# Score products of neighbouring units issued in turn in the second block's mixers

## The chip, the cores and the metric

The program runs on one core of a Trainium2 chip. Its metric is the device time of one execution, in microseconds; the median of the runs is compared. TensorE (PE in the profile) does the matrix products, VectorE (DVE) and ScalarE (ACT) the elementwise work, GpSimd (POOL) very little, and SyncE (SP) issues the DMAs of the weights.

## What is computed

A row block x of 256 tokens by 1024 features goes through two model blocks of two layers each. The first block (a stick-breaking and gated linear mixer, then a routed set of experts) isn't touched by the change. The second block does, for each of its two layers:

```
h    = rms_norm(x) * gain
proj = h @ w_in                                   # split into the inputs of four branches
y_a  = latent attention, 4 heads of 64+32         # softmax over 256 keys
y_b  = differential attention, 4 heads, two softmaxes each, w = p0 - lam * p1
y_c  = banded attention with sinks, 4 query heads
y_d  = neighbourhood attention with a bias table, 4 heads
x    = x + concat(norm(y_a), y_b, norm(y_c), norm(y_d)) @ w_out
x    = x + square(relu(rms_norm(x) @ w_up)) @ w_down
```

Everything is fp32. The large products are done as three products of values split into a high and a low part (fp32r); the products of the attentions are plain fp32 products. The profile shows a plain one as two pairs of weight load and matmul, called two passes below.

## The kernel before

All weights stream once through a ring of four slots of 1 MB. ScalarE copies each slot's tile to a rounded high part (line 926 inside the mixers) and VectorE subtracts it from the raw tile to get the low part (line 935); TensorE waits for the low part. Three split tiles are held, so a split waits until the tile three before it has been used.

The attention of a layer of the second block ("mix2") is cut into 20 **units**, each with 128 queries, 256 keys and two heads (branches A, C and D) or the two softmaxes of one head (branch B). A unit is written here as its branch, its p and its i, so B01 is branch B, p = 0, query half i = 1. The units in order (B00, B01, B10, ... B31, A00, ... A11, C00, ... C11, D00, ... D11) are dealt to three **lanes** in turn, and each lane has its own PSUM bank and its own buffers; a unit starts only when the one before it in its lane has been written out.

The steps of a unit are, on TensorE, **S** (two score products of 128 queries by 256 keys, lines 1861 to 1863), **T** (transposes of the probabilities, line 1871) and **V** (the products with v, line 1877); on ScalarE **exp** (line 2005) and **cpT** (the copy of the transposes, line 2011); on VectorE **max** (lines 2162 to 2171: mask, row maximum, scaling), **rec** (line 2175 to 2183: reciprocals, for B the difference of the softmaxes) and **y** (line 2191, for B line 2188: the output of the unit).

The contraction of a score product is over 64 rows in the branches B, C and D, and over 96 in A. With 64 rows it lies in rows 0 to 63 of the array if p is even and in rows 64 to 127 if p is odd, because `rows64 = slice(64 * p, 64 * p + 64)`, and `slice(64 * (p % 2), ...)` for B.

When the units of a branch are done, its **fin** steps run. For branch C these are facC on ScalarE (line 2069: squares, then a logarithm and an exponential that make the norm's factor), finC2 on VectorE (line 2264: the branch times its factor), finC.T on TensorE (line 1957: transposes), turnC on ScalarE (line 2081: the high part of the transposed branch) and finC3 on VectorE (line 2269: its low part). The output projection runs in four tiles out2.0 to out2.3, each in two halves c0 and c1 (line 1840, 12 matmuls each half). out2.0 takes branch B, out2.1 branch A, out2.2 branch C, and out2.3 branch D. A tile's first half waits for the fin3 step of its branch: `pe.wait_ge(v_ms, 19 * l + (11, 16, 18, 19)[t])`. The input projection runs in the steps in2.0 to in2.5 (lines 1792 and 1816), and the steps named mla (lines 1912 to 1929) lift the queries and keys of branch A.

Each engine executes its instructions in program order. For TensorE, ScalarE and VectorE that order is written out by hand: a string of digits for each layer and engine, in which each digit says which of several generators goes on to its next `yield`. The digits 1 to 3 are the three lanes, 0 and 4 (and 5) the projection, the fin steps and the weight splits.

```python
def steps(order, *lanes):

    live = dict(enumerate(lanes))
    for q in [int(q) for q in order]:
        if q in live and next(live[q], 0) == 0:
            del live[q]
```

Of the kernel before, what the change touches and what calls it, by code (L numbers as in the profile page):

```python
# [12 lines left out]
ACT = mybir.ActivationFunctionType  # L13
# [11 lines left out]
IN1 = (0, 1, 3, 2, 4, 5)  # L25
ORDER = {("mix1", 0, "PE"): "00400400066550500556650155301535005500515534505314540151315050543510455510404545050055044500000", ("mix1", 0, "ACT"): "0000040660004056645103500061563500543100153113156000135051005640040504400", ("mix1", 0, "DVE"): "00006006040606664065666510630004650031040513141600450044004653415400440044500",
# [3 lines left out]


def layout(parts):
# [86 lines left out]
def program(nc, a, out):  # L119
    ctx = ExitStack()  # L120
    with ctx:
# [1728 lines left out]
        def pe_units(pe, l, L):  # L1850
            for n, u in enumerate(L.units):
                at = len(L.units) * l + n
                if n:
                    pe.wait_ge(L.vector, 3 * at)
                if n == 0 or L.units[n - 1].br != u.br:
                    pe.wait_ge(v_ms, 19 * l + {"A": 8, "B": 3, "C": 14, "D": 9}[u.br])
                    pe.wait_ge(a_ev, 6 * l + {"A": 2, "B": 3, "C": 3, "D": 6}[u.br])
                    pe.wait_ge(v_ev, 10 * l + {"A": 5, "B": 3, "C": 3, "D": 10}[u.br])
                    if u.br == "A":
                        pe.wait_ge(a_ms, 13 * l + 5)  # L1860
                for j, (q, k) in enumerate(u.qk):
                    ins = pe.matmul(ps[:, L.b, 256 * j:256 * j + 256], q, k, start=True, stop=True)  # L1862
                ins.then_inc(L.psum, 1)
                yield
                if u.br == "B":
                    pe.wait_ge(L.vector, 3 * at + 2)
                else:
                    pe.wait_ge(L.scalar, 2 * at + 1)
                for j in range(len(u.vs)):
                    for kt in range(2):  # L1870
                        ins = pe.transpose(ps[:, L.b, 256 * j + 128 * kt:256 * j + 128 * kt + 128], L.pt[:, j, 128 * kt:128 * kt + 128], ident)  # L1871
                ins.then_inc(L.psum, 1)
                yield
                pe.wait_ge(L.scalar, 2 * at + 2)
                for j, c in enumerate(u.vs):
                    for kt in range(2):
                        ins = pe.matmul(ps[:, L.b, 64 * j:64 * j + 64], L.ptT[:, j, kt, :], m2.v[:, kt, c:c + 64], start=(kt == 0), stop=(kt == 1))  # L1877
                ins.then_inc(L.psum, 1)
                yield
# [83 lines left out]
        def pe_mix2(pe, g, l):  # L1963
            pe_x_T(pe, 4 + 2 * l)
            if l == 0:
                pe_spin(pe, 6, 2)
            steps(ORDER["mix2", l, "PE"], pe_main2(pe, g, l), *(pe_units(pe, l, L) for L in LANES), pe_misc2(pe, l))
# [654 lines left out]
```

## Time and profile before

| what | value |
|---|---|
| median of 3 runs | 1470.93 us (1469.54 to 1472.16) |
| profiled execution: its own time | 1464.29 us |
| profiled execution: span of the core | 1462.1 us |
| busy: PE, PEld, DVE, ACT, POOL | 1317.6, 983.6, 729.3, 526.4, 49.6 us |
| mean granted TensorE clock | 0.960 |
| mixer of layer 0 of the second block | some 122 us, from 827 to 949 us |
| mixer of layer 1 of the second block | some 124 us, from 1149 to 1273 us |

Times are microseconds from the first instruction. A matmul's end in the profile is modelled, since matmuls are pipelined: the time that a step takes of TensorE is read from the first start in it to the first start in the next step, not from its length. PEld is the weight load that goes ahead of each matmul. A name such as "ps<-ar" says which tile is written and which are read; "ar" is the common scratch area, and "gate" holds, in the branch B, the keys of the second softmax.

### The profile page before, as it was taken

To read this page: it belongs to the slowest core of one execution; us is meant where nothing else is said; L and a number is where in the kernel's file an instruction comes from. 1 tells how busy PE (TensorE), PEld (TensorE's weight loads), DVE (VectorE), ACT (ScalarE), POOL (GpSimd) and SP (SyncE) were. 2 spreads that over 40 slices of the span, in tenths; PEclk is the share of its full clock that TensorE was granted. 3 is DMA by queue.
4 is the path that set the end of the run, shared out by engine and by line. 5 is a ranking of instruction groups with operands and counts; after the bars stand their busy time and mean duration, and the time that the engine had idled before them with its cause. 6 is when DMAs were issued, how large, how long until landed. Compare 5 with 4: busy or idle time off the path is not lost. (4 is left out here: it accounts for less than half of the span.)

```text
span 1462.1 us, 21540 instructions
## 1 busy us (share of the span) xinstructions
PE 1317.6 (90%) x9066; PEld 983.6 (67%) x9066; DVE 729.3 (50%) x1126; ACT 526.4 (36%) x894; POOL 49.6 (3%) x46
## 2 busy tenths in 40 slices
PE   5999998867689999976776999999999999999997
PEld 2766774433247667643432878799988978799996
DVE  1744653122157367421111878764554777755454
ACT  3545331000045344200001546554444546644343
POOL 0200000000002000000000110000000110000000
PEclk9999999889899999998888999999999999999999
DMA  9799899999977958999999705446655404455550
GB/s 354 284 332 312 334 403 420 421 422 421 419 278 285 337 188 331 421 421 421 421 421 402 187 6 202 146 154 209 191 187 150 108 32 171 144 174 200 180 200 39
DMA packets 135975, 392.08 MB, mean 268 GB/s; under 512 B 26816, under 2 KB 40128, under 8 KB 111296
## 3 DMA queue, kind: packets, MB, share of 16 engines
q1 hardware_dynamic: 132128, 389.48, 71.5%
q10 hardware_dynamic: 3744, 1.15, 0.4%
q8 instruction: 75, 1.23, 0.3%
q14 instruction: 28, 0.23, 0.0%
HBM read 389.45 MB, written 1.05 MB: 267 GB/s over the span
## 5 line engine op out<-in xcount | busy, mean ns | idle before, releaser
L421 DVE TENSOR_TENSOR spl<-ring,spl 128x2048 fp32r<-128x2048 f32 x65 | 149.0, 2292 | 135.7 <-ACT spl L412 135.7
L545 PEld LDWEIGHTS ps<-hh,spl 128*128 128x128 f32 x1728 | 204.1, 189 | 6.9 <-issue 5.8
L545 PE MATMUL ps<-hh,spl 128*128 128x256 f32 x1728 | 206.2, 281 | 2.8 <-DVE hh L507 2.8
L412 ACT ACTIVATE spl<-ring 128x2048 fp32r<-128x2048 f32 x66 | 126.6, 1919 | 148.1 <-PE ps L545 107.7
L2349 PE MATMUL ps<-spl,ur 128*128 128x512 f32 x768 | 176.7, 389 | 0.0
L1348 PE MATMUL ps<-ring,ar 128*32 128x256 f32 x960 | 112.7, 486 | 63.3 <-DMA spl_as_slots<-in_w_up 28.6
L2349 PEld LDWEIGHTS ps<-spl,ur 128*128 128x128 f32 x768 | 143.2, 188 | 29.2
L935 DVE TENSOR_TENSOR spl<-ring,spl 128x1024 fp32r<-128x1024 f32 (+2 forms) x120 | 138.2, 1175 | 23.0 <-ACT spl L926 22.6
L1348 PE MATMUL ps<-spl_as_slots,ar 128*32 128x256 f32 x736 | 110.5, 486 | 28.3 <-DMA spl_as_slots<-in_w_up 17.3
L926 ACT ACTIVATE spl<-ring 128x1024 fp32r<-128x1024 f32 (+2 forms) x120 | 116.7, 1010 | 43.3 <-PE ps L525 10.7
L1348 PEld LDWEIGHTS ps<-ring,ar 128*32 128x32 f32 x960 | 54.7, 139 | 101.9 <-issue 95.7
L525 PE MATMUL ps<-spl,hh 128*128 128x512 f32 x480 | 117.6, 398 | 3.6 <-DVE hh L1048 1.3
L1561 DVE TENSOR_TENSOR ar<-ps,ar 128x256 f32<-128x256 f32 x16 | 6.8, 425 | 220.1 <-ACT ar L1437 220.1
L525 PEld LDWEIGHTS ps<-spl,hh 128*128 128x128 f32 x480 | 88.4, 188 | 32.0 <-issue 12.2
L1437 ACT ACTIVATE ar<-ps 128x256 f32<-128x256 f32 x16 | 6.1, 383 | 276.6 <-PE ps L1348 276.6
L1348 PEld LDWEIGHTS ps<-spl_as_slots,ar 128*32 128x32 f32 x736 | 52.5, 139 | 52.8 <-issue 44.7
L1816 PE MATMUL ps<-hh,spl 128*128 128x256 f32 (+1 forms) x672 | 86.0, 286 | 2.0 <-DVE hh L507 1.9
L1816 PEld LDWEIGHTS ps<-hh,spl 128*128 128x128 f32 (+1 forms) x672 | 81.2, 191 | 6.9 <-issue 6.0
L1393 PE MATMUL ps<-spl_as_slots,ar 128*32 128x512 f32 x400 | 58.1, 594 | 10.0 <-ACT ar L1450 8.1
L606 PE MATMUL ps<-ring,ccol 128*32 128x512 f32 x384 | 52.1, 639 | 14.9 <-DMA ring<-in_w_ada 14.9
L1413 PE MATMUL ps<-gate,hh_as_floats 128*128 128x512 f32 x128 | 63.0, 614 | 1.9 <-ACT hh_as_floats L1446 1.7
L1339 PE MATMUL ps<-ar,xn 128*128 128x256 f32 (+1 forms) x320 | 58.3, 340 | 0.0
(370 smaller groups left out, 1787.8 us busy)
## 6 DMA issues: line engine op xcount, KB each, us to landing
ring<-in_w_up SPq DMA_DIRECT2D x58, 1024.0 KB, 5.8
spl_as_slots<-in_w_down SPq DMA_DIRECT2D x50, 1024.0 KB, 16.8
ring<-in_w_ada SPq DMA_DIRECT2D x48, 1024.0 KB, 7.1
ring<-in_w_down SPq DMA_DIRECT2D x40, 1024.0 KB, 4.9
ring<-in_w_in SPq DMA_DIRECT2D x34, 1024.0 KB, 7.5
ring<-in_w_gate SPq DMA_DIRECT2D x34, 1024.0 KB, 15.9
spl_as_slots<-in_w_up SPq DMA_DIRECT2D x30, 1024.0 KB, 16.7
ring<-in_w_out SPq DMA_DIRECT2D x16, 1024.0 KB, 7.7
```

The source lines that it names most:

```text
L412: sc.activation(t.hi, t.raw, ACT.Copy).then_inc(s_hi, 2)
L421: v.tensor_tensor(t.lo, t.raw, t.hi, ALU.subtract).then_inc(s_lo, 1)
L525: ins = pe.matmul(ps[:, banks[i], 0:cn], le, ri, start=(kk == 0 and q == 0), stop=(kk == 7 and q == 2), skip_group_check=True)
L545: ins = pe.matmul(ps[:, banks[m // 2], (m % 2) * 256:(m % 2) * 256 + 256], le, ri, start=(kk == 0 and q == 0 and m % 2 == 0), stop=(kk == ...
L926: sc.activation(t.hi[:, h], t.raw[:, h], ACT.Copy).then_inc(s_hi, 1)
L935: ins = v.tensor_tensor(t.lo[:, h], t.raw[:, h], t.hi[:, h], ALU.subtract)
L1339: ins = pe.matmul(slots_out(c, k), xn[:, i, 128 * k:128 * k + 128], mo.pr[:, i, s0:s0 + n], start=(i == 0), stop=(i == 1), skip_group_chec ...
L1348: ins = pe.matmul(ps[32 * j:32 * j + 32, 2 + q % 2, 256 * z:256 * z + 256], mo.xg[c][:, k, CAP * e - CHUNKS[c][0]:CAP * e - CHUNKS[c][0] + ...
L1393: ins = pe.matmul(ps[32 * j:32 * j + 32, c, :], mo.aT[q % 2][:, f, 32 * j:32 * j + 32], T["down", l, 4 * q + j].raw[:, f, 512 * c:512 * c ...
L1413: pe.matmul(ps[:, 6 + m % 2, :], mo.pT[:, q, 128 * i:128 * i + 128], mo.ys[:, 512 * c:512 * c + 512], start=True, stop=True).then_inc(s_b, 1)
L1816: ins = pe.matmul(o, le, ri, start=(kk == 0 and q == 0 and m % 2 == 0), stop=(kk == 7 and q == 2), skip_group_check=True)
L2349: ins = pe.matmul(ps[:, 2 * cc + i, :], le, ri, start=(d == 0 and f2 == 0 and f == 0 and q == 0), stop=(d == 7 and f2 == 1 and f == 1 and ...
```

## The change

A unit's S step gets two yields in place of one, so that another generator can come between its two score products. The semaphore that VectorE waits for is still raised by the second product alone.

```diff
                 for j, (q, k) in enumerate(u.qk):
                     ins = pe.matmul(ps[:, L.b, 256 * j:256 * j + 256], q, k, start=True, stop=True)
-                ins.then_inc(L.psum, 1)
-                yield
+                    if j:
+                        ins.then_inc(L.psum, 1)
+                    yield
```

The strings of the two layers get the extra digits for TensorE. In four places of each layer two units of opposite rows then follow each other in turn: B01 with B10, B30 with B21, C10 with D00, and D10 with D01. Everywhere else s0 and s1 of a unit stay together. Decoded into steps, these are the places where the order differs (s0 and s1 are the two products of S; the rest of the order is the same in both kernels):

```
layer 0, PE, before: B00.S B01.S B10.S in2.2
             after:  B00.s0 B00.s1 B01.s0 B10.s0 B01.s1 B10.s1 in2.2
         before: mla.q B30.S B20.T B21.S mla.qperm
         after:  mla.q B30.s0 B21.s0 B30.s1 B21.s1 B20.T mla.qperm
         before: C11.T C10.S C11.V finA.T D00.S out2.0c0 out2.0c1 D00.T C10.T D10.S C10.V
                 out2.1c0 D10.T D01.S D00.V D10.V D11.S finC.T out2.1c1 D01.T out2.2c0 out2.2c1
                 D11.T D01.V D11.V finD.T out2.3
         after:  C11.T C10.s0 D00.s0 C10.s1 D00.s1 C11.V finA.T out2.0c0 out2.0c1 D00.T C10.T
                 out2.1c0 C10.V D00.V D10.s0 D01.s0 D10.s1 D01.s1 out2.1c1 D10.T D11.s0 D11.s1
                 D10.V finC.T out2.2c0 D01.T out2.2c1 D11.T D01.V D11.V finD.T out2.3
layer 0, ACT, before: D00.cpT split D10.exp split D10.cpT facC D01.exp turnC split D11.exp
             after:   D00.cpT split split D10.exp D01.exp D10.cpT facC turnC split D11.exp
layer 0, DVE, before: C10.rec D10.max split D00.rec C10.y D01.max D00.y finC2 D11.max finC3
             after:   C10.rec split D00.rec C10.y D00.y D10.max D01.max finC2 D11.max finC3
layer 1, PE, before: B00.S B01.S B10.S in2.2
             after:  B00.s0 B00.s1 B01.s0 B10.s0 B01.s1 B10.s1 in2.2
         before: B10.V B30.S B20.T B21.S B20.V mla.qperm
         after:  B10.V B20.T B30.s0 B21.s0 B30.s1 B21.s1 B20.V mla.qperm
         before: C11.T C10.S D00.S C11.V finA.T out2.0c0 out2.0c1 D10.S C10.T D00.T
                 out2.1c0 C10.V D00.V D01.S out2.1c1 D10.T finC.T D11.S D10.V D01.T out2.2c0
         after:  C11.T C10.s0 D00.s0 C10.s1 D00.s1 C11.V finA.T out2.0c0 out2.0c1 C10.T D00.T
                 out2.1c0 C10.V D00.V D10.s0 D01.s0 D10.s1 D01.s1 out2.1c1 D10.T finC.T D11.s0
                 D11.s1 D10.V D01.T out2.2c0
layer 1, ACT, before: D00.exp split C10.cpT D10.exp D00.cpT facC split D01.exp D10.cpT turnC
             after:   D00.exp split C10.cpT D00.cpT facC split D10.exp D01.exp D10.cpT turnC
layer 1, DVE, before: C10.rec split D10.max split C10.y D00.rec D10.rec D00.y D01.max finC2 split finC3
             after:   C10.rec split split D00.rec C10.y D00.y D10.max D01.max D10.rec finC2 split finC3
```

## Rows read from the trace of the kernel before

**Rows 1.** The page's first part: busy us (share of the span) and instructions.

```profile
PE 1317.6 (90%) x9066; PEld 983.6 (67%) x9066; DVE 729.3 (50%) x1126; ACT 526.4 (36%) x894; POOL 49.6 (3%) x46
```

**Rows 2.** Stretches, both mixers: busy us (x) by engine, PEclk, DMA share, GB/s.

```profile
826.90:949.50 122.60, 120.46 (x753) 101.16 (x752) 93.50 (x197) 66.82 (x173) 6.47 (x5) 0.99 0.40 128
1149.00:1273.00 124.00, 121.16 (x755) 101.60 (x754) 94.46 (x198) 67.76 (x173) 6.33 (x5) 0.99 0.38 124
```

**Rows 3.** Timeline of PE, layer 0, B00, B01, B10: start, us, engine line op.

```profile
834.97 0.70 PE L1862 MATMUL ps<-ar 64*128 64x256 f32 x2
...
835.93 0.70 PE L1862 MATMUL ps<-ar 64*128 64x256 f32 x4
836.37 0.70 PE L1862 MATMUL ps<-gate,ar 64*128 64x256 f32 x4
837.00 4.40 PE L1816 MATMUL ps<-hh,spl 128*128 128x256 f32 x36
```

**Rows 4.** Timeline of PE, layer 0, B21.S and mla.qperm.

```profile
861.04 0.70 PE L1862 MATMUL ps<-ar 64*128 64x256 f32 x2
...
862.09 1.91 PE L1919 MATMUL ps<-ar 32*32 32x256 f32 x8
```

**Rows 5.** Timeline of PE, layer 0, from C10.S to D11.T.

```profile
909.58 1.13 PE L1862 MATMUL ps<-ar 64*128 64x256 f32 x4
910.63 1.10 PE L1877 MATMUL ps<-ar,xn 128*128 128x64 f32 x8
...
913.17 5.74 PE L1840 MATMUL ps<-spl,ur 128*128 128x512 f32 x24
918.75 0.60 PE L1871 MATMUL ps<-cst,xn 128*128 128x128 f32 x4
...
926.12 2.00 PE L1877 MATMUL ps<-ar,xn 128*128 128x64 f32 x16
...
929.24 0.66 PE L1957 MATMUL ps<-cst,gate 128*128 128x128 f32 x4
...
932.86 5.74 PE L1840 MATMUL ps<-spl,hh 128*128 128x512 f32 x24
938.44 0.60 PE L1871 MATMUL ps<-cst,xn 128*128 128x128 f32 x4
```

**Rows 6.** Timeline of DVE, layer 0: C01.y, D10.max's first, finC2, finC3.

```profile
910.60 0.28 DVE L2191 TENSOR_TENSOR gate<-ps,st 128x128 f32<-128x128 f32 x1
...
920.96 0.69 DVE L2162 SCALAR_TENSOR_TENSOR xn<-ps,ar 128x512 f32<-128x512 f32 x1 [2.48 <-PE ps L1862]
...
928.04 0.68 DVE L2264 TENSOR_TENSOR gate<-gate,st 128x512 f32<-128x512 f32 x1
...
930.87 0.87 DVE L2269 SCALAR_TENSOR_TENSOR hh<-ps,prm,hh 128x256 fp32r<-128x256 f32 x2
```

**Rows 7.** Timeline of ACT, layer 0: D10.exp, D10.cpT, end of facC, turnC.

```profile
922.61 0.51 ACT L2005 ACTIVATE xn<-xn,st 128x256 f32<-128x256 f32 x1 [0.76 <-DVE st L2171]
...
923.52 0.19 ACT L2005 ACTIVATION_READ_ACCUMULATOR xn<-xn,st 128x1 f32 x1
...
925.17 0.60 ACT L2011 ACTIVATE xn<-ps 128x512 f32<-128x512 f32 x1 [0.52 <-PE ps L1871]
...
926.92 0.20 ACT L2072 ACTIVATE st<-st 128x2 f32<-128x2 f32 x1
...
929.93 0.84 ACT L2081 ACTIVATE hh<-ps,prm 128x256 fp32r<-128x256 f32 x2 [0.89 <-PE ps L1957]
```

**Rows 8.** Timeline of PE, layer 1: C10.S with D00.S, finC.T, out2.2c0.

```profile
1234.28 1.55 PE L1862 MATMUL ps<-ar 64*128 64x256 f32 x8
...
1253.67 0.60 PE L1957 MATMUL ps<-cst,gate 128*128 128x128 f32 x4
...
1256.56 3.01 PE L1840 MATMUL ps<-spl,hh 128*128 128x512 f32 x12
```

**Rows 9.** A stretch of layer 0, columns as in Rows 2.

```profile
864.11:867.52 3.41, 3.37 (x16) 3.18 (x16) 3.30 (x5) 0.80 (x3) 3.29 (x2) 0.50 0.00 0
```

4 rows, old and new, of the table ORDER are left out of this document.

## The prediction

> **What bounds the kernel now.** I read the page's busy times first: TensorE is busy for 90% of the span, VectorE for 50% [rows 1]. Then the view by stretches, for the two mixers alone: TensorE is busy for 120.5 of 122.6 us and for 121.2 of 124 us, at a granted clock of 0.99, with the DMA engines at 0.4 [rows 2]. So a microsecond taken off TensorE's order in a mixer shortens the kernel, as long as the next step's input is there, and everything after the mixer moves up with it. "As long as" is the whole question here, so the rest is read from the timelines of the three engines: when each step starts, and what it waits for.
>
> **What a pair is worth.** A lone S step holds TensorE for 1.06 us from its first start to the next step's (861.04 to 862.09, 909.58 to 910.63) [rows 4, 5]: four passes at 0.216 and the change back to the whole array. Coming in costs some 0.1 more. Now look at the first pair of layer 0. B01 (rows 0 to 63) and B10 (rows 64 to 127) stand one behind the other in the program, four passes each. The timeline has them as four "ps<-ar" in one row and four "ps<-gate,ar" in the next, though the program has two, two, two, two; all eight take 1.07 us (835.93 to 837.00) [rows 3]. So the array already runs two neighbouring S steps of opposite rows side by side, without being given them in turn. A second S joined to a first costs about 0.1 us and saves the 1.06 and its 0.1, about 1.04 us.
>
> The Trainium skill (TensorE: Matmul & The Clock Gate, Part 3, The mechanism) says that matmuls start and end in program order, and that only tiles next to each other overlap. By that rule B10 could begin only with B01's last pass, and taking them in turn would be what brings the overlap. The row of this trace says otherwise. What the rule would make of the time stands as a rival below.
>
> **Pair by pair.** Of the eight places, B01/B10 in both layers are neighbours already: 0. C10/D00 of layer 1 are neighbours too, eight passes in 1.48 us to the next step (row of 1.55) [rows 8]: D00 comes in late there because it waits for the last input projection to be copied, and it still will: 0. B30/B21 of layer 1, now parted by B20.T: 1.04 saved. B30/B21 of layer 0: B30 runs beside mla.q already, so the pair saves only B21's way into and out of the 64-row mode, 0.3 us. VectorE's longest wait behind it, for GpSimd on the rotation of the queries, starts from mla.qperm and moves with it. D10/D01, parted in both layers: 1.04 each, before waits.
>
> C10/D00 of layer 0 is the first trap. D00 needs C01.y, its lane's unit before, and that stands on VectorE behind two splits and finA2: it ends at 910.88 [rows 6]. Today C10.S (909.58), C11.V and finA.T fill that time and D00 starts at 912.12. In the new order D00.s0 is asked for at 910.0, waits until about 911.05, and C10.s1, C11.V and finA.T wait behind it. From there: four passes 1.06, then C11.V and finA.T 1.31 (913.17 minus 910.63, less D00's 1.06 and 0.17 of changes). out2.0 starts at 913.4 against 913.17 [rows 5]: 0.24 lost where 1.04 was to be had. C10.max ends 0.75 later, and C10.exp with it, but out2.0 (5.58 us) covers both.
>
> **The end of layer 0, step by step.** out2.0 ends and D00.T begins at 919.0 (918.75 before) [rows 5]. Without D10.S behind it out2.1c0 starts at 919.8 and ends at 922.7; (12 of the 24 matmuls of 5.58 us); C10.V and D00.V take 1.8 (16 matmuls, the row of 2.00 less the overhang of the last) [rows 5], so the pair D10/D01 starts at 924.5, and C10.y, which D01 waits for, is written during D00.V. It takes 1.17; out2.1c1 runs from 925.7 to 928.5, D10.T to 929.1, D11.S to 930.1.
>
> Meanwhile the chain: D10's scores are there at 925.65. max, from 920.96 to the start of exp at 922.61, takes 1.62 [rows 6, 7], and both units' maxima now come one after the other: 928.8. D10.exp took 922.61 to 923.71 [rows 7], so D10.T isn't late, but ScalarE then has D01.exp (928.9 to 930.0) ahead of D10.cpT, and facC behind that. D10.V starts at 930.5 instead of 930.1. From D10.cpT's start to the end of facC are 1.95 us (925.17 to 927.12) [rows 7]: facC ends at 931.8, finC2 (0.68) [rows 6] at 932.5, and finC.T starts at 932.6, 1.1 us after D10.V has ended. Before, facC ran under D01.S and the V steps and was off the path.
>
> The next step in the new order is out2.2c0, which needs finC3. From finC.T's start to finC3's end are 2.50 us (929.24 to 931.74, with turnC from 929.93) [rows 5 to 7]. Today out2.1c1 and D01.T stand between them and hide it. Now nothing does: out2.2c0 starts at 935.1 against 932.86, TensorE idle for 2.1 us. D01.T's 0.35 comes inside out2.2 now and not before it, so D11.T is at 941.1 against 938.44 [rows 5]. From D11.T on the two orders are equal. Loss 2.7, less the 0.3 of B30/B21: **layer 0 is 2.4 us longer**.
>
> **Layer 1.** Here facC stands ahead of D10.exp, and finC.T has D11.S, D10.V and D01.T between it and out2.2c0. From the pair's start: max twice 4.3, then D10.rec and finC2 5.05; TensorE arrives at finC.T after 1.17 + 2.85 (out2.1c1) + 0.45 (D10.T) = 4.5 and waits 0.6. The rest keeps its distances (2.9 us from 1253.67 to 1256.56 cover finC3) [rows 8]. So the last pair yields 0.46, with B30/B21's 1.04: **layer 1 is 1.5 us shorter**. Sum of both: +0.9 us.
>
> **The clock.** In layer 0 TensorE would have 1.35 us of work between 930.1 and 935.1. The trace has a fall of the granted clock from 1.00 to 0.50, 1.2 GHz, for 3.41 us in the mixer of layer 0 [rows 9], and layer 1's mean of 0.99 [rows 2] comes from one of the same length; it comes with TensorE never idle before it, only working on 64 and 32 rows (B21.S and mla.qperm) [rows 4]. The three waits would leave it less to do than that, so I expect a fall there too. Its bounds: 0 if it doesn't come or ends before out2.2c0, 1.7 us if 3.41 us of matmuls run at half rate. I take 1.2, nearer the upper end, since the fall would come late in the idle time. The existing falls may go away where the pair B30/B21 gives more load before them; in layer 0 that gains nothing, because B21.T waits for VectorE right behind it, in layer 1 up to 0.7. I take 0.
>
> The sum is +2.1 us: the profiled execution would go from 1464.3 (span 1462.1 and 2.2 around it) to 1466.4. The runs' median is 6.6 us above that execution; added to it the forecast is **1473.0 us**. I take 0.2%, 2.9 us, as what can be told from no change.
>
> **Rivals.**
> 1. *The chain of branch C does not bite.* If facC, finC2 and finC3 came as fast behind the pair as they do today, layer 0 would keep 0.3 and 1.04 less 0.24, layer 1 2.08: 3.2 us less, and with C01.y early enough for C10/D00 4.5: 1467. For it: the order was free of such waits before. Against it: 2.50 us of finC latency have no other step of TensorE beside them. Chance 0.12.
> 2. *The clock falls and stays down* (slower). Place: out2.2 of layer 0. If the half rate begins near 935 and lasts twice as long as the one in the rows, out2.2 loses 3.4 us: +4.3, 1475.5. It decides from a fall that reaches beyond 938. For it: only 1.35 of 5 us are work. Against: dense matmuls follow. Chance 0.22.
> 3. *Only taking in turn overlaps*, the rule above. Then B01/B10 ran in 1.5 us before and take 1.0 after, half a microsecond in each layer and 0.3 for C10/D00 of layer 1: 1.3 less than my sum, 1471.7. The 1.07 us for eight passes speak plainly against it. Chance 0.04.
> 4. *In turn blocks*: s1 of the one behind s0 of the other, or two rows' matmuls that hold each other up. Then the pairs in turn take two lone steps, 2.1 us, in all eight places: 5 us more than forecast, 1478. Nothing in the rows speaks for it. Chance 0.05.
>
> The forecast's own case has 0.57; its range is 1470.8 (no fall, gains a little larger) to 1475. The range that should hold the time 8 times in 10 goes from rival 1's 1467 to 1477, which takes in rival 2 with the waits mis-sized by 1 us. Faster by over 0.2%: rival 1 and a little of the rest, 0.13. Slower by over 0.2% means over 1473.9: rivals 2 and 4 and a fourth of my own case, 0.37. Same: 0.50.
>
> **What would show it.** Right: lone S steps in branch B to D fewer by five, with 8 passes in 1.07 to 1.2 us in their place; C10.S of layer 0 torn in two by a wait for VectorE line 2191; TensorE waiting for line 2264 before finC.T and over 2 us for line 2269 before out2.2c0, in layer 0 only; layer 0's mixer longer, layer 1's shorter by 1.5. Wrong: out2.2c0 of layer 0 starting right behind finC.T; the first pairs shorter than 1.07; layer 1 unchanged (then VectorE bounds it); or a granted clock that stays at 1.00 around 935.

## The result, and the profile after

Fourteen runs of each kernel, taken side by side: 1471.67 us (median; 1468.68 to 1477.62) with the change, 1468.76 (1462.27 to 1472.16) without. The ratio is 1.0031 [1.0021, 1.0041], so the change costs 4.6 us [3.1, 6.0]: slower by over 0.2% by that ratio. The two medians are closer, 2.9 us or 0.20% apart. The forecast of 1473.0 stood on a median of 1470.93 and a loss of 2.1 us; it lies 1.3 us above the measured median, because the base was 2.2 us too high and the loss, by the medians, 0.8 too small. The profiled executions took 1468.68 (span 1466.5) and 1464.29 us (span 1462.1), 4.4 apart; both are from the fast end of their kernel's executions.

The busy times hardly move, beside [rows 1]:

```profile
PE 1315.2 (90%) x9066; PEld 980.2 (67%) x9066; DVE 730.6 (50%) x1126; ACT 526.2 (36%) x894; POOL 49.9 (3%) x46
```

TensorE works 2.4 us less and the span is 4.4 us longer, so TensorE waits 6.8 us more in all. (A matmul that runs at half the clock counts as busy, so the busy time hides what the clock costs.) Where the loss lies, the starts of steps in both timelines tell (us; each column from one step's first start to the next one's; "first S" is B00's first score product, "A" the first score product of branch A, "MLP" the first matmul of the stage behind the mixer, line 545):

```
                 first S -> A -> out2.0 -> out2.2 -> out2.3 -> MLP      all
before  layer 0     42.68   35.53    19.69    11.11    9.05       118.06
after   layer 0     44.74   35.85    22.13    13.44    9.02       125.18
before  layer 1     44.59   34.63    19.49    11.54    9.01       119.27
after   layer 1     43.34   34.62    19.12    11.54    9.03       117.65
```

Layer 0 loses 7.1, layer 1 gains 1.6, and the blocks before, which the change doesn't touch, happened to end 1.1 earlier. The view by stretches of the kernel after has the same stages (columns as in [rows 2]):

```profile
833.87:878.61 44.74, 41.27 (x270) 34.03 (x269) 33.43 (x74) 19.11 (x54) 6.52 (x5) 0.96 0.10 28
914.46:936.59 22.13, 18.84 (x103) 14.97 (x102) 13.33 (x30) 11.84 (x34) 0.00 (x0) 0.94 0.30 96
936.59:950.04 13.45, 12.65 (x57) 9.71 (x57) 7.73 (x12) 7.72 (x17) 0.00 (x0) 0.85 0.45 153
933.80:940.60 6.80, 4.87 (x14) 3.66 (x14) 4.77 (x10) 2.76 (x7) 0.00 (x0) 0.50 0.05 7
```

Read the last one first: from 933.80 TensorE's granted clock is at 0.50, its lower level of 1.2 GHz, twice as long as in [rows 9]. The two stretches above it hold 3.3 and 0.8 us in which TensorE does nothing; [rows 2] had 2.1 in a whole mixer.

The end of layer 0, in TensorE's timeline (start, us, operation, what the wait before it was for), against [rows 5]:

```profile
910.75 0.70 PE L1862 MATMUL ps<-ar 64*128 64x256 f32 x2
912.10 1.13 PE L1862 MATMUL ps<-ar 64*128 64x256 f32 x6 [0.65 <-DVE gate L2192]
...
914.46 5.73 PE L1840 MATMUL ps<-spl,ur 128*128 128x512 f32 x24
...
925.46 1.13 PE L1862 MATMUL ps<-ar 64*128 64x256 f32 x8
926.53 3.02 PE L1840 MATMUL ps<-spl,ur 128*128 128x512 f32 x12
...
931.51 1.10 PE L1878 MATMUL ps<-ar,xn 128*128 128x64 f32 x8 [0.29 <-ACT xn L2012]
...
933.69 0.97 PE L1958 MATMUL ps<-cst,gate 128*128 128x128 f32 x4 [1.07 <-DVE gate L2265]
936.59 4.88 PE L1840 MATMUL ps<-spl,hh 128*128 128x512 f32 x12 [1.93 <-DVE hh L2270]
```

C10.S is torn in two by the wait for C01.y, the pair D10/D01 takes 1.07 us for its eight passes, D10.V waits for D10.cpT, finC.T for finC2 (line 2265) and out2.2c0 for finC3 (line 2270). Every wait of the forecast is there, at its place. Then out2.2c0 takes 4.72 us to the next step for what takes 2.85 at the higher clock.

The other place is the end of branch B, which the forecast had at nothing. TensorE, VectorE and GpSimd in layer 0:

```profile
863.86 0.55 PE L1878 MATMUL ps<-ar,xn 128*128 128x64 f32 x4
867.45 0.44 PE L1872 MATMUL ps<-cst,ar 128*128 128x128 f32 x2 [3.03 <-DVE ar L2184]
```

```profile
862.31 0.35 DVE L2183 TENSOR_SCALAR xn<-xn,st 128x256 f32<-128x256 f32 x1
862.70 2.56 DVE L2184 SCALAR_TENSOR_TENSOR xn<-xn,st 128x256 f32<-128x256 f32 x1
...
866.30 1.10 DVE L2184 SCALAR_TENSOR_TENSOR ar<-ar,st 128x256 f32<-128x256 f32 x1
```

```profile
862.61 2.37 POOL L2318 TENSOR_TENSOR ar<-ar 32x1024 f32<-32x1024 f32 x1 [44.44 <-PE ps L1920]
```

B30's last softmax step on VectorE takes 2.56 us. It began 0.09 us after GpSimd's first step on the rotation of the queries, and ends 0.3 after that step's end. In the kernel before it began 0.31 us ahead of GpSimd and took 0.48, and a step of B21 was caught instead:

```profile
863.84 0.48 DVE L2183 SCALAR_TENSOR_TENSOR xn<-xn,st 128x256 f32<-128x256 f32 x1
...
864.68 2.02 DVE L2182 TENSOR_SCALAR ar<-ar,st 128x256 f32<-128x256 f32 x1
```

```profile
864.15 2.41 POOL L2317 TENSOR_TENSOR ar<-ar 32x1024 f32<-32x1024 f32 x1 [44.88 <-PE ps L1919]
```

There TensorE's B21.T waited 0.49 us, where it waits 3.03 after:

```profile
867.97 0.44 PE L1871 MATMUL ps<-cst,ar 128*128 128x128 f32 x2 [0.49 <-DVE ar L2183]
```

In both kernels VectorE started second, and its step ended 0.1 to 0.3 us behind the end of GpSimd's. The Trainium skill (SBUF — State Buffer, Who interferes with whom) says so: the two engines share a pair of ports that one instruction holds to its end, and "Issue order, not op shape, decides who blocks". The rows agree for VectorE. The other way round they don't show a full stop: GpSimd's step, started while VectorE's had 0.17 us left, took 2.41 us against 2.37 (times on GpSimd are rough).

### The profile page after: what moved, and what is told of

The parts are those of the page before. It is cut to its first block and busy times, and to the rows that moved or that the text cites. A ratio compares the mean times of both kernels' runs of the same rounds, so it can differ in the third digit from the quotient of the medians.

```text
span 1466.5 us, 21540 instructions
## 1 busy us (share of the span) xinstructions
PE 1315.2 (90%) x9066; PEld 980.2 (67%) x9066; DVE 730.6 (50%) x1126; ACT 526.2 (36%) x894; POOL 49.9 (3%) x46
## 5 line engine op out<-in xcount | busy, mean ns | idle before, releaser
L525 PE MATMUL ps<-spl,hh 128*128 128x512 f32 x480 | 117.7, 398 | 2.8 <-DVE spl L935 1.5
```

The costliest lines, as they stand in the source:

```text
L525: ins = pe.matmul(ps[:, banks[i], 0:cn], le, ri, start=(kk == 0 and q == 0), stop=(kk == 7 and q == 2), skip_group_check=True)
```

## The experiments

Each is timed against the kernel before on the same chip; a ratio is given with its 95% interval. Stages are those of the table above.

**The change again, and one layer at a time.** `a1_after` is the changed kernel. The other two give one layer its old sequences (s0 and s1 of a unit in one step):

```
 a2_layer0_only:  ("mix2", 1, "PE"/"ACT"/"DVE"): as before;  layer 0 as after
 a3_layer1_only:  ("mix2", 0, "PE"/"ACT"/"DVE"): as before;  layer 1 as after
```

> The changed kernel once more, beside the kernel before on the same chip, as the base for the three others. My theory (the sum by stages of the two profiles): the first mixer is 5 to 7 us longer, the second 1.6 us shorter, nothing else moves; so 1.0031 again, within 0.001. The rival, that a part of the 4.4 us was where the clock happened to fall in one execution: then the first mixer comes out at 3 to 4 us longer in this profile and the falls of the clock stand elsewhere.

> Layer 0 has the new order, layer 1 the order of the kernel before (s0 and s1 of every unit together). My theory: layer 0's mixer alone is what costs, so 5 to 7 us longer than before, ratio 1.003 to 1.005, and longer than the whole change by 1 to 2 us. Rival (the loss is spread, or noise of the chip): no slower than the whole change.

> Layer 1 has the new order, layer 0 the order of the kernel before. My theory: layer 1's mixer is shorter by 1.4 to 1.7 us and nothing else changes, ratio 0.9990, the mixer of layer 0 at 118 us as before. Rival (VectorE bounds the mixer of layer 1, and the 1.6 us of the first profile came from a fall of the clock that was missing there): layer 1's mixer within 0.5 us of before when the clock falls in it as before.

Measured: a1 1471.92 us, 1.0030 [1.0017, 1.0043]; a2 1472.41, 1.0026 [1.0014, 1.0038]; a3 1467.63, 0.9989 [0.9977, 1.0002]. Layer 0 carries the whole loss; what layer 1 gains isn't told from nothing by its time. Layer 0's mixer was 8.1 us longer than before in a1's profile and 8.6 in a2's, more than the 5 to 7 expected, and a2 wasn't slower than the whole change, though that had been expected; a3's layer 1 was 1.5 us shorter, as expected. The traces of a2 and a3 tell more. Here is branch B of the two layers in a3, then in a2, columns as in [rows 2]:

```profile
834.16:876.74 42.58, 40.14 (x269) 32.69 (x269) 32.83 (x75) 19.21 (x54) 6.46 (x5) 1.00 0.11 30
1157.10:1200.51 43.41, 40.88 (x269) 32.81 (x269) 34.31 (x76) 19.22 (x54) 6.55 (x5) 1.00 0.08 25
```

```profile
836.27:882.45 46.18, 42.71 (x270) 34.91 (x269) 33.44 (x74) 19.11 (x54) 6.51 (x5) 0.93 0.09 26
1167.76:1210.76 43.00, 41.83 (x269) 33.41 (x269) 34.18 (x76) 19.36 (x54) 6.44 (x5) 1.00 0.08 25
```

Layer 1 in its old order takes 43.00 us at a clock of 1.00, and 44.59 in the kernel before, where the clock fell for 3.41 us. In the new order it takes 43.41. So the new order of branch B, with B30 and B21 joined, gains nothing there, it costs 0.4; what the kernel after gained is that the fall stayed away. In layer 0 the fall lasted 6.83 us in a2, and branch B took 46.18.

**Joined, not in turn.** All pairs stand as after, but one unit's two halves ahead of the other's:

```
-D10.s0 D01.s0 D10.s1 D01.s1
+D10.s0 D10.s1 D01.s0 D01.s1      (and so the other seven places)
```

> The order of the change in all eight places, but the two units of a pair one behind the other and not in turn: s0 s1 of the one, then s0 s1 of the other. My theory (the array runs neighbours of opposite rows side by side whatever their turn): a pair still takes under 1.25 us for its eight passes, 0.1 more than in turn, and the time is that of the change within 1 us. A second point of it: with the in-turn order the first unit's scores are signalled only when the partner's first product has ended; here B30's signal in layer 0 comes 0.39 us after its last pass starts, and VectorE's B30 steps end before GpSimd's long instruction begins. The rival, the skill's rule (TensorE: Matmul & The Clock Gate, Part 3, The mechanism), says only neighbours in program order overlap: then each of the pairs takes 1.5 us or more, and the time is 3 us over that of the change.

Measured: 1472.48 us, 1.0021 [1.0008, 1.0035]; the stages after branch B are those of a1 within 0.4 us up to out2.3 (35.87 against 35.48 from out2.0). Taking the pairs in turn gives nothing that can be told apart. In branch B of layer 0 B30's step escaped (VectorE, then GpSimd), which isolates one half of the story:

```profile
866.05 0.48 DVE L2184 SCALAR_TENSOR_TENSOR xn<-xn,st 128x256 f32<-128x256 f32 x1
...
866.89 2.01 DVE L2183 TENSOR_SCALAR ar<-ar,st 128x256 f32<-128x256 f32 x1
```

```profile
866.30 2.45 POOL L2318 TENSOR_TENSOR ar<-ar 32x1024 f32<-32x1024 f32 x1 [44.59 <-PE ps L1920]
```

And yet branch B took 45.53 us: the clock was at half for 6.83 us behind it. The collision of B30's step isn't the only thing that made layer 0 longer, and a late fall of the clock doesn't need it.

**Filling the waits.** TensorE multiplies constants into an unused bank while it waits, in layer 0's end only:

```
+ if l == 0 and t == 2: pe_spin(pe, 5, 2)       # behind V(D10), ahead of finC.T's wait
+ if l == 0 and br == "C": pe.wait_ge(LANES[2].vector, 16); pe_spin(pe, 5, 1)   # ahead of out2.2c0
```

> The changed kernel, with idle work for TensorE in the two waits of layer 0's end: one plain fp32 product of 512 columns into the free bank of lane 2 ahead of finC.T, two ahead of out2.2c0. The wait stays as it was. My theory (the fall of the clock for 6.83 us is the answer to those waits): the clock stays at 1.00 there, out2.2c0 takes 2.85 us and not 4.7, and the kernel is 1.7 to 2.1 us faster than the change; the fall in branch B of layer 0 stays. Rival (the clock falls for the sum of what lies before, or the idle work delays out2.2c0 itself): no gain over 0.5 us.

Measured: 1471.55 us, 1.0023 [1.0013, 1.0034]. At this place the clock stayed at 1.00:

```profile
918.99:940.61 21.62, 21.14 (x110) 15.64 (x108) 13.26 (x30) 11.76 (x34) 0.00 (x0) 1.00 0.31 98
940.61:952.19 11.58, 10.78 (x57) 8.30 (x57) 7.81 (x14) 7.81 (x17) 0.00 (x0) 1.00 0.54 177
```

The two stretches are 33.20 us against 35.57 after: 2.4 us of the loss are the clock, 0.5 ahead of out2.2c0 and 1.9 in it. The waits stay: finC.T began at 938.11, out2.2c0 2.50 us behind it, the forecast's own figure. From A to the MLP it took 78.1 us against 75.4 before, 2.7 us more. So the trace shows the gain and the times don't: 1.0023 isn't told from the change's 1.0030 (a1), where 1.7 to 2.1 us less were expected. This run's branch B of layer 0 took 46.07 us, with a fall of 6.83.

**The queries' rotation made small.** GpSimd's step that VectorE met works on four elements of each row instead of 1024, so this kernel leaves out most of the rotation:

```
-po.tensor_tensor(m2.qm[r, :, :], m2.qm[r, :, :], bc(TB("cos32")[r, :], 1, 4), ALU.mult)
+po.tensor_tensor(m2.qm[r, :, 0:1], m2.qm[r, :, 0:1], bc(TB("cos32")[r, 0:1], 1, 4), ALU.mult)
```

> The changed kernel, with GpSimd's multiplication of the queries of branch A by the cosines cut to the first of 256 columns in both layers (the rest is left out, so the queries of A aren't rotated in full). My theory (that instruction of 2.4 us holds back VectorE's step for B30, which started 0.08 us in layer 0 and 0.12 us in layer 1 behind it): the B30 step of VectorE takes 0.48 us and not 2.56, the wait before the next transposes shrinks by 2 us, and from the first score product to branch A's first it takes 41 to 42.5 us in layer 0 (44.7 in the change) and 41.5 to 42.3 in layer 1 (43.3). Rival (VectorE's own queue and not GpSimd is the limit there): both stretches within 0.5 us of the change.

Measured: 1467.28 us, 0.9997 [0.9983, 1.0010]. VectorE's step takes its 0.49 us, 0.09 behind a GpSimd step of 0.20:

```profile
865.87 0.49 DVE L2184 SCALAR_TENSOR_TENSOR xn<-xn,st 128x256 f32<-128x256 f32 x1
```

```profile
865.78 0.20 POOL L2318 TENSOR_TENSOR ar<-ar 32x4 f32<-32x4 f32 x1 [44.45 <-PE ps L1920]
```

```profile
837.02:879.77 42.75, 41.33 (x269) 34.15 (x269) 31.37 (x74) 19.11 (x54) 4.46 (x5) 0.96 0.10 28
1165.39:1207.25 41.86, 40.58 (x269) 32.70 (x269) 32.28 (x76) 19.18 (x54) 4.52 (x5) 1.00 0.09 26
```

Branch B is 2.0 us shorter in layer 0 than after (42.75, just above the 41 to 42.5 expected, with a fall of 3.41 us in it) and 1.5 in layer 1, where the clock is at 1.00 in both kernels. So the collision costs time in both layers. Against layer 1's old order the gain is 43.00 less 41.86, 1.1 us, but that isn't the price of the pair alone: the old order has a collision too, of a step of B21, which started 0.18 us behind GpSimd's (in the kernel before):

```profile
1189.41 2.47 DVE L2183 SCALAR_TENSOR_TENSOR ar<-ar,st 128x256 f32<-128x256 f32 x1
```

**The two places of layer 0 alone.** In b3 only B30/B21 change, in b4 only what stands from branch A on:

```
 b3, PE, layer 0:  -B30.s0 B30.s1 B20.T B21.s0 B21.s1   +B30.s0 B21.s0 B30.s1 B21.s1 B20.T
 b4, layer 0:      sequences of before up to A01, of after from A01 on;  layer 1 as before in both
```

> The kernel before, with nothing but the pair B30/B21 of layer 0 in turn. My theory: the pair takes the wait out of TensorE but puts B30's step of VectorE behind GpSimd's; B21.T starts 0.5 to 0.7 us later, and the clock falls behind the wait: branch B of layer 0 is 1.5 to 3.5 us longer than before, layer 1 as before, time 1.5 to 3 us more. Rival (my prediction's first reading): 0.3 us less.

> The kernel before, with the new order of layer 0 from branch A on only (C10/D00, D10/D01 and the end of the layer on three engines). My theory: from out2.0 to the first product of the next stage it takes 44.4 us and not 39.9, 2.6 of the 4.6 from the two waits of branch C's norm and 1.9 from the clock; time 4.5 to 5 us more than before. Rival (the loss of the change is in branch B): under 2.5 us more.

Measured: b3 1469.31 us, 1.0011 [0.9999, 1.0022], branch B of layer 0 44.86; b4 1472.90, 1.0036 [1.0024, 1.0048]. b3 is within what was expected; b4's stretch took the 44.4 us expected, its time 5.3 us more by the ratio, a little over the 4.5 to 5. In b3 the one pair brings the collision, and the fall lies behind it:

```profile
864.34 2.56 DVE L2184 SCALAR_TENSOR_TENSOR xn<-xn,st 128x256 f32<-128x256 f32 x1
```

```profile
870.40:873.81 3.41, 3.41 (x15) 2.82 (x14) 2.22 (x5) 1.20 (x6) 0.44 (x1) 0.50 0.00 0
```

In b4 branch B stays at 42.74 and the end comes with its waits and its fall:

```profile
914.97:937.23 22.26, 18.96 (x103) 15.09 (x102) 13.33 (x30) 11.87 (x34) 0.00 (x0) 0.92 0.31 95
933.70:940.53 6.83, 4.38 (x12) 3.37 (x13) 5.39 (x11) 2.77 (x7) 0.00 (x0) 0.50 0.00 0
```

From out2.0 to out2.3 it takes 35.36 against 30.80 before, 4.6 us. After the change it is 35.57, 4.8 more. So of the 7.1 us of layer 0, 4.8 are the end, 0.3 the place of C10/D00 ahead of it and 2.1 branch B; the end and branch B show alone about what they show together (4.6 and 2.2).

**Another order for layer 0.** Three recombinations of sequences that exist already, and the old one of layer 1 twice, as a control:

```
 c1:  layer 0's three sequences = layer 1's new ones
 c2:  both layers: before's layer 0 up to A01, layer 1's new ones from A01 on
 c3:  c2 with B01 and B10 in turn
 d1:  both layers = layer 1's old ones (those of the kernel before)
```

> The changed kernel, but layer 0 runs in layer 1's new order on all three engines: the same four pairs, facC ahead of D10.exp on ScalarE, and D11.S, D10.V and D01.T between finC.T and out2.2c0. My theory (layer 0's loss at its end is the order of branch C's norm, not the pairs): out2.0 to the next stage 39.7 us as in layer 1 (44.5 in the change), no fall of the clock there, both mixers at 117.5 to 118 us, and the time 1 to 2.5 us under the kernel before. Rival (something of layer 0 itself, such as its weights' splits, makes the wait): over 42 us from out2.0 on.

> In both layers: layer 0's order of the kernel before up to branch A, without any pair in turn in branch B, and layer 1's new order from branch A on (C10/D00 and D10/D01 in turn). Theory, from the stretches of single profiles: 42.6 + 34.6 + 39.7 = 116.9 us for each mixer, against 118.1 and 119.3, so 3.3 us less, ratio 0.9978. Rival (the gain of layer 1's new order is only that the clock doesn't fall in branch B): then this kernel has the fall again in branch B, at 28 to 31 us after the first score product, and each mixer takes 118 us or more.

> As the one before, and B01 with B10 in turn in both layers. Theory: taking in turn saves 0.11 us for each of the two (B10's first pass starts beside B00's third and not beside B01's first), and the rest of branch B moves up with it if VectorE's B30 step still starts ahead of GpSimd's; so the same time within 0.3 us. Rival: the shift puts that step behind GpSimd's, and branch B takes 43.3 us or more.

> Both layers in layer 1's order of the kernel before: no pair in turn, C10/D00 and B01/B10 neighbours as before. It tells how much of the gain of the kernel with layer 1's new order in both layers is that order and how much the pairs. My theory: each mixer takes 119.2 us where the clock falls in branch B (44.6 us to branch A) and 117.7 us where it doesn't (43.0), and it falls in most executions, so the time is 0 to 1.5 us over the kernel before, ratio 1.0000 to 1.0010, against 0.9974. Rival (the new order's pairs bring nothing, and the layer's order alone made the 0.9974): ratio below 0.9985, both mixers at 117.7 us.

```
                     us      ratio [95%]              first S -> A, layers 0, 1 (fall of the clock, us)
c1 new l1 twice   1464.01   0.9974 [0.9960, 0.9989]   43.34 (none)   43.41 (none)
c2 recombined     1466.90   0.9992 [0.9977, 1.0007]   42.70 (none)   44.14 (3.4)
c3 B01/B10 too    1466.92   0.9998 [0.9982, 1.0013]   45.64 (6.8)    45.65 (6.8)
d1 old l1 twice   1466.65   1.0008 [0.9991, 1.0024]   43.04 (none)   44.55 (3.4)
```

c1 beats both kernels: 0.26% faster than before, 3.8 us by the ratio, of which its profile accounts for 1.9 (mixers of 117.7 and 117.7 us against 118.1 and 119.3). Its stretches are those expected; its time had been expected 1 to 2.5 us lower. Its layer 0, branch B and out2.0 to out2.2, shows a clock that never falls, and at the end 0.50 us of waiting, all of it finC.T's:

```profile
836.32:879.66 43.34, 40.78 (x269) 32.72 (x269) 34.32 (x76) 19.21 (x54) 6.55 (x5) 1.00 0.11 29
914.28:933.40 19.12, 18.62 (x108) 15.10 (x106) 13.66 (x31) 13.14 (x35) 0.00 (x0) 1.00 0.37 110
```

```profile
930.48 0.63 PE L1958 MATMUL ps<-cst,gate 128*128 128x128 f32 x4 [0.50 <-DVE gate L2265]
931.04 1.13 PE L1862 MATMUL ps<-ar 64*128 64x256 f32 x4
932.09 1.10 PE L1878 MATMUL ps<-ar,xn 128*128 128x64 f32 x8
933.04 0.61 PE L1872 MATMUL ps<-cst,ar 128*128 128x128 f32 x4
933.40 1.86 PE L1840 MATMUL ps<-spl,hh 128*128 128x512 f32 x7
```

D11.S, D10.V and D01.T stand between finC.T and out2.2c0 and hide finC3, which layer 0's new order had taken away. d1 is not told from before, so c1's gain is not that layer 0 runs in layer 1's order but that this order is the new one. (The last row of c1's view is cut off by its window.) c2 and c3, which keep the old start of layer 0, have falls again, and c2 missed its 0.9978: its mixers took 117.0 and 118.5 us. In c3 branch B takes 2.9 and 1.5 us more than in c2, with one pair put in turn. The rival named a collision for that, and there is none of B30's step: it started 0.31 us ahead of GpSimd's in both layers and took 0.48. The difference is the fall alone, and the times of the two kernels are the same (1466.92 and 1466.90), so single profiles don't show that the pair brings it. TensorE was busy through the whole fall:

```profile
870.70:877.53 6.83, 6.83 (x28) 6.00 (x27) 4.44 (x9) 1.84 (x7) 1.90 (x2) 0.50 0.01 2
```

## Why the prediction was right, and where it was wrong

**The waits at the end of layer 0: right.** C10/D00 cost 0.3 us (0.24 forecast; the stage from A to out2.0 took 35.53 to 35.74 us in three profiles of the old order and 35.66 to 35.86 in seven of the new, 0.2 on average). finC.T waited 1.07 after D10.V (1.1), out2.2c0 began 21.62 us behind out2.0 in b1 and 22.13 after (21.7), and layer 0 from A on, with the clock kept up, was 2.7 us longer in b1, as forecast. A wait could be worked out to a tenth from the durations in the rows of the three engines and the order alone.

**The clock behind those waits: the right mechanism, mis-sized.** "Its bounds: 0 [...] 1.7 us if 3.41 us of matmuls run at half rate. I take 1.2" failed: the fall lasted 6.83 us in all six profiles with this end and nothing to fill its waits (in the kernel after from 933.8 to 940.6), and cost 2.4 us (b1 against after). The length was read from the one fall in [rows 9]. Rival 2, a fall twice as long that reaches beyond 938 and had a chance of 0.22, is what happened (by its own sum it stood at 1475.2, not 1475.5); its price of 3.4 was too high because the fall began 1.2 us earlier, in the wait, and so spent 2.8 of its 6.8 us before out2.2c0.

**B30/B21 of layer 0: wrong.** The forecast was that the pair saves 0.3 and that VectorE's wait for GpSimd "starts from mla.qperm and moves with it". It cost 2.1 us in this profile and 2.2 in b3. What moved was one of two: from first S, GpSimd's step came 0.44 us earlier (28.74 against 29.18), VectorE's step of B30 stayed (28.83 against 28.87). That put them in the other order. B30's step then took 2.56 us, B21's steps behind it ended late, and B21.T started 33.58 us after first S instead of 33.00: 0.6. The rest is the clock. The old fall lay from 29.1 to 32.5 us, ahead of a wait for VectorE, where it cost 0.1 us at most: with it (before) branch B took 42.68, without it (a3) 42.58. The new one, of the same length, came at 35.1, behind the wait, and stretched the next 24 dense matmuls: 4.45 us for 3.03, 1.4 us. 0.6 and 1.4 are 2.0 of the 2.1. The collision is shown to be the cause of its part: b2 takes it away, b3 brings it alone, and in after, a1, a2 and b1 B30's step starts 0.09 us behind GpSimd's each time. The clock's part is less sure. In a1, a2 and b1, with the same layer 0 in branch B, the fall lasted 6.8 to 10.2 us and branch B took 45.8 to 46.2, so the 2.1 of this profile is the low end. A fall that reaches into the dense matmuls came in all five profiles with B30/B21 in turn and the full rotation, but also in a4, b2 and c3 without B30's collision, and in one of five mixers with the old order (c2's layer 1, 44.14 us). No run fills the wait in branch B, so that the collision brings the late fall there is argued and not shown.

**B30/B21 of layer 1: wrong.** "1.04 saved" wasn't earned. With the clock at 1.00 the old order took 43.00 and 43.04 (a2, d1), the new one 43.34 to 43.44: 0.3 to 0.4 lost. Here VectorE's step of B30 (1193.90) met GpSimd's (1193.79) as well:

```profile
1193.90 2.52 DVE L2184 SCALAR_TENSOR_TENSOR xn<-xn,st 128x256 f32<-128x256 f32 x1
```

```profile
1196.48 0.44 PE L1872 MATMUL ps<-cst,xn 128*128 128x128 f32 x2 [1.27 <-DVE xn L2184]
```

b2 shows what was hidden: 1.5 us of layer 1's branch B hang on that collision. The forecast compared the old order with the new as if neither met GpSimd; both do.

**Layer 1's sum came out right by luck.** Forecast -1.5, measured -1.6. Of it 0.37 is the last pair (0.46 forecast). The other 1.25 is a fall of the clock that went away, worth 1.6 (44.59 against 43.00), less the 0.4 of the collision. The forecast's "in layer 1 up to 0.7. I take 0" was too low. The fall came in 4 of 6 mixers in layer 1's old order (before, b3, b4, d1's layer 1; not in a2 nor d1's layer 0) and in none of 8 in its new one (a4 counted, where the pairs are joined and not in turn). What in the new order keeps it away wasn't isolated.

**In turn against joined: right.** Pairs that were neighbours gained 0.1 us at most (below). Rival 3's rule, by which taking in turn brings the overlap, and rival 4, by which it blocks, both fall with the 1.07 us that the pair D10/D01 takes in either form (925.46 to 926.53 after, 929.78 to 930.85 in a4). That only neighbouring steps overlap was the prediction's own conclusion from the order of starts. Rival 1 fell with the waits.

**The sum, and luck.** Forecast +2.1 in two layers; the traces have +5.5 there (+7.1 and -1.6) and +4.4 with the earlier blocks, the runs +4.6. Of the 3.4 us by which the forecast of the two layers was short, 2.4 are B30/B21 of layer 0 (+2.1 for -0.3) and 1.2 the clock at its end, less 0.1 of layer 1. The three terms are from single profiled executions; how long a fall in branch B lasts differed between executions of the same code (3.4 us after, 10.2 in a1), and by a1's profile the two layers would have lost 6.6 us (+8.1 and -1.5). That the absolute time came within 1.3 us of 1473.0 is luck: the base of three runs was 2.2 us above the later median of fourteen, which more than made up for a loss forecast too small, by 0.8 us by the medians and by 2.5 by the ratio. The outcome thought most likely, no change over 0.2% (0.50), lost to "slower" (0.37), by the ratio.

## What to carry to other kernels

Where one engine's step holds up another's, as GpSimd's did VectorE's here, a step that costs 0.5 us costs 2.5 if it starts 0.1 us too late; before an order is changed, list for each such pair which starts first and by how much, since a saving of 0.3 us upstream can turn it. A wait of TensorE costs twice where dense matmuls follow: once as idle time, and again as half rate, here 2.4 us on top of 2.7; put small steps that are ready between a step whose result goes round over other engines and the dense work that needs it. And look whether a fall of the clock lies ahead of a wait for another engine, where it cost 0.1 us at most here, or behind it, before giving it a price.

## What the runs showed of the hardware

**How the array takes two row halves.** D10/D01, in turn, went from first start to the next step in 1.07 us, all eight passes two by two, with 7 ns at most inside a couple: exactly a lone step, where 1.17 was forecast. Joined and not in turn it took the same in a4:

```profile
929.78 1.14 PE L1862 MATMUL ps<-ar 64*128 64x256 f32 x8
930.85 1.89 PE L1840 MATMUL ps<-spl,ur 128*128 128x512 f32 x7
```

Where a third unit stands in front, in turn was worth 0.11: B00, B01 and B10 take 833.87 to 835.79 after, 834.97 to 837.00 before [rows 3]. There B10's first pass starts beside B00's third, ahead of B00's fourth and of B01's first two, which stand before it in the program (the semaphores that they raise tell the units apart: B10's last pass starts at 835.17, B01's at 835.49):

```profile
834.41 0.38 PE L1862 MATMUL ps<-gate,ar 64*128 64x256 f32 x1
834.41 0.48 PE L1862 MATMUL ps<-ar 64*128 64x256 f32 x1
```

The Trainium skill (TensorE: Matmul & The Clock Gate, Part 3, The mechanism) has matmuls start strictly in program order; for two row halves these rows say otherwise.

**Completions seem to be told in program order.** In layer 0 B30's scores were free for VectorE 0.73 us after B30's last pass had started, when B21's first half, ahead of it in the program, had ended; elsewhere it is 0.39. From first S, VectorE's step of B30 came at 28.83 in turn and at 28.64 in a4, joined but not in turn, and there it was ahead of GpSimd's, by 0.25 us. A second case is B10 in layer 0 of the kernel after: its last pass started at 835.17 and its semaphore rose 0.75 us later, 0.04 behind that of B01, which stands ahead of it in the program and whose last pass started only at 835.49. That the order of completions is the cause is read from these times and wasn't tried by itself.
